# Second block of a two-block kernel: halves of turned columns between products, an output product by tiles, and masks between query copies

## The reference

```python
n = _rmsnorm(h, attn_norm[l])
p = n @ w_in                       # token-shifted part, latents, gates
y_a = _rwkv7_time_mix(...) @ w_out_rwkv
y_b = _mla(q_lat, kv_lat, k_pe, ...) @ w_out_mla
merged = jax.nn.sigmoid(gate_a) * y_a + jax.nn.sigmoid(gate_b) * y_b
h = h + merged @ w_out
n = _rmsnorm(h, ffn_norm[l])
h = h + (jax.nn.gelu(conv(n @ w_up_gate)) * (n @ w_up_val)) @ w_ffn_down
```

## Time and profile before

| | |
|---|---|
| median of 3 runs | 2201.04 us (2199.91 to 2202.91) |
| the profiled execution | 2207.04 us, span 2205.2 us |
| TensorE busy | 1902.1 us (86%) |
| VectorE, ScalarE, GpSimd busy | 914.9 (41%), 739.1 (34%), 40.5 (2%) us |
| weights and the rest read | 592 MB, mean 269 GB/s |
| mean granted TensorE clock | 0.945 |

### The profile page before, as it was taken

How to read it: one execution, slowest core, us unless ns; L and a number is a source line. 1 busy time by engine, 2 the same in 40 slices (tenths; PEclk the granted TensorE clock), 3 DMA queues, 4 the chain that set the end, 5 groups by cost and what they waited for, 6 DMA issues and landing times.

```text
span 2205.2 us, 37736 instructions
## 1 busy us (share of the span) xinstructions
PE 1902.1 (86%) x16684; PEld 1289.0 (58%) x16684; DVE 914.9 (41%) x1316; ACT 739.1 (34%) x1043; POOL 40.5 (2%) x65
## 2 busy tenths in 40 slices
PE   7999976667769999876666679999999999999998
PEld 6897322222218896322122239677899885778996
DVE  6445211111106454110110127457677474476774
ACT  5444211111106453211111125425444453264442
POOL 1000000000001000000000000000000000000000
PEclk9999988888889999988888889999999999999999
DMA  9346999999997257999999996022853450237540
GB/s 331 114 154 270 421 428 429 428 429 429 428 418 292 77 191 321 428 428 429 428 428 429 429 404 216 4 105 102 265 189 136 141 201 4 79 115 246 184 174 20
DMA packets 141523, 592.34 MB, mean 269 GB/s; under 512 B 5808, under 2 KB 59264, under 8 KB 116560
## 3 DMA queue, kind: packets, MB, share of 16 engines
q1 hardware_dynamic: 140288, 586.68, 67.1%
q0 software_dynamic: 1104, 3.70, 0.5%
HBM read 589.30 MB, written 1.05 MB: 268 GB/s over the span
## 4 chain that ended last, share of the span: by engine, by line
PE 68%; DMA 24%; DVE 4%; ACT 2%; issue 1%; SPq 1%; DVEq 0%; POOLq 0%; ACTq 0%; POOL 0%
PE ps L600 38%; DMA ring<-in_w_up 24%; PE ps L1269 12%; PE ps L2394 3%; PE ps L939 2%; PE ps L2443 1%; PE ps L1295 1%; PE ps L1305 1%; PE ps L617 1%; DVE ring_lo L576 1%; PE ps L1045 1%; PE ps L1124 1%; PE ps L1149 1%; SPq L808 1%; ACT slab_hi L571 1%
## 5 line engine op out<-in xcount | busy, mean ns | idle before, releaser
L1269 PE MATMUL ps<-ring,area 128*32 128x512 f32 x1888 | 311.0, 726 | 202.2 <-DMA ring<-in_w_up 202.2
L576 DVE TENSOR_TENSOR ring_lo<-ring,slab_hi 128x2048 fp32r<-128x2048 f32 (+1 forms) x138 | 312.0, 2261 | 217.1 <-ACT slab_hi L571 217.0
L571 ACT ACTIVATE slab_hi<-ring 128x2048 fp32r<-128x2048 f32 (+1 forms) x138 | 260.6, 1888 | 274.9 <-PE ps L600 258.6
L1269 PEld LDWEIGHTS ps<-ring,area 128*32 128x32 f32 x1888 | 72.0, 130 | 403.2 <-DMA ring<-in_w_up 233.6
L600 PE MATMUL ps<-hT_hi,slab_hi 128*128 128x256 f32 x832 | 234.4, 282 | 1.6 <-DVE hT_lo L593 1.6
L600 PE MATMUL ps<-hT_hi,ring_lo 128*128 128x256 f32 x832 | 232.9, 280 | 0.0
L600 PE MATMUL ps<-hT_lo,slab_hi 128*128 128x256 f32 x832 | 232.7, 280 | 0.0
L1541 ACT ACTIVATE area<-ps 128x512 f32<-128x512 f32 x32 | 19.1, 597 | 615.2 <-PE ps L1269 615.2
L1917 DVE COPY area<-ps 128x256 f32<-128x256 f32 x32 | 13.6, 425 | 459.0 <-PE ps L1213 459.0
L1295 PE MATMUL ps<-ring,area 128*32 128x512 f32 x992 | 120.0, 606 | 49.7 <-DVE area L1939 32.5
L600 PEld LDWEIGHTS ps<-hT_hi,slab_hi 128*128 128x128 f32 x832 | 156.6, 188 | 2.0 <-DVE hT_lo L593 2.0
(11 more groups left out here) (428 smaller groups left out, 3199.4 us busy)
## 6 DMA issues: line engine op xcount, KB each, us to landing
ring<-in_w_up SPq DMA_DIRECT2D x60, 2048.0 KB, 20.5
ring<-in_w_down SPq DMA_DIRECT2D x60, 2048.0 KB, 25.4
ring<-in_w_gate SPq DMA_DIRECT2D x56, 2048.0 KB, 15.1
ring<-in_w_ffn_up SPq DMA_DIRECT2D x44, 1024.0 KB, 7.8
ring<-in_w_in SPq DMA_DIRECT2D x18, 2048.0 KB, 10.2
ring<-in_w_ffn_down SPq DMA_DIRECT2D x10, 2048.0 KB, 7.8
ring<-in_xattn_w_kv SPq DMA_DIRECT2D x8, 2048.0 KB, 16.8
area<-in_w_gate SPq DMA_DIRECT2D x6, 2048.0 KB, 16.7
```

Source lines behind the costliest of these rows:

```text
L571: return m.nc.scalar.activation(hi, whole, ACT.Copy)
L576: return m.nc.vector.tensor_tensor(lo, whole, hi, ALU.subtract)
L1269: ins = mm(ps[32 * g:32 * g + CAP, 1, :], m.tokT[:, k, :], gate_up[i][:, k % 4, (g % 2) * BANK:(g % 2 + 1) * BANK], start=k == 0, stop=k = ...
```

## The change

It affects only the second block.

1. **Masks.** The four mask copies (with their wait for `bonus_in`) go from behind the squares to between the second and the third query copy on ScalarE.
2. **Branch.** The second branch product (`w_out_rwkv`) is done tile by tile (both contraction halves of one tile, then the next), where before the tiles of the two halves were interleaved at the start.
3. **Merged.** Half 0 of the merged rows is turned before tile 3 of the branch, half 1 between the two token tiles of the first out product. VectorE makes the low columns of half 0 between the third and the fourth merge, and does its low part of the second out half slab ahead of all merges. `merged_T` and `merged_cols_d` get semaphores of their own.
4. **n2.** Half 1 is turned inside the first up product, which is now done in quarters: c = 0 with columns 0 to 3, turning, c = 1 with columns 0 to 3, then c = 0 and c = 1 with columns 4 to 7. It waits column by column. ScalarE does its second high half slab between the column halves.
5. **n1 of layer 1.** Half 0 is turned before the last tile of the last down product of layer 0; half 1 inside the first input product, by the `first_tiles` that layer 0 has. VectorE's low columns of half 0 stand before the last addition into x. `n1_lo` moves to another area, and the slot of the last down slab is given up with half 1.

```diff
@@ allocate
-    m.n1_lo = over("n1_lo", area_at, after_lat + PAIRS * T, KD, T)
+    m.n1_lo = over("n1_lo", extra_at, SLAB // 2, KD, T)
@@ second_columns
-               freed=m.free[PLAN2[W_DN + NDN - 1].slot] if l and half == 0 else None)
+               freed=m.free[PLAN2[W_DN + NDN - 1].slot] if l and half == 1 else None)
@@ tensor_second
-    if l:
-        for half in range(2):
-            second_columns(m, pe, l, half)
...
-        if l == 0 and q == 0:
+        if q == 0:
             first_tiles()
...
-    for h, i in ((0, 0), (0, 1), (1, 0), (1, 1), (0, 2), (1, 2), (0, 3), (1, 3)):
-        if h == 1 and i == 0:
-            pe.wait_ge(*at("branch_lo", l, 4))
-        branch(0, h, i, (m.ya_hi, m.ya_lo))
+    for i in range(4):
+        if i == 3:
+            merged_columns(0)
+        for h in range(2):
+            if i == 0 and h == 1:
+                pe.wait_ge(*at("branch_lo", l, 4))
+            branch(0, h, i, (m.ya_hi, m.ya_lo))
     release.append(W_ORW)
-    for half in range(2):
-        pe.wait_ge(*at("merged", l, 2 * (half + 1)))
-        pe_columns(m, m.xn, s("merged_T"), (2 * half, 2 * half + 1))
...
+            if j == 0 and t == 1:
+                merged_columns(1)
...
-    pe.wait_ge(*at("h_mixed", l))
-    pe_columns(m, m.x, s("n2_T"), (2, 3))
+    def first_up():
+
+        pe.wait_ge(*at("w_lo", l, 1))
+        w = [a.rearrange("p (k n) -> p k n", k=KD) for a in ffn_half(m, l, 0)[:2]]
+        for half in range(2):
+            for c in range(2):
+                if c and half == 0:
+                    pe.wait_ge(*at("h_mixed", l))
+                    pe_columns(m, m.x, s("n2_T"), (2, 3))
+                for k in range(4 * half, 4 * half + 4):
+                    if c == 0:
+                        pe.wait_ge(*at("n2_cols_d", l, k + 1))
+                    first, ins = exact(m, half_bank(m, up_bank(0, 0), c), [a[:, k, c * P:(c + 1) * P] for a in w],
+                                       [a[:, k, :] for a in columns], c == 0 and k == 0, k == KD - 1, skip_group_check=True)
+                    free_released(first)
+        ins.then_inc(s("up_full"), 1)
...
+            if l + 1 < L and r == NF // 2 - 1 and b == order[-1]:
+                second_columns(m, pe, l + 1, 0)
@@ scalar_second
+        if i == 2:
+            masks()
         act.wait_ge(*at("q2_full", l, i + 1))
...
-    act_high_columns(m, act, m.hT_hi, m.par2("ffn_g"), *at("n2_T", l, 0), s("n2_cols_a"))
+    act_high_columns(m, act, m.hT_hi, m.par2("ffn_g"), *at("n2_T", l, 0), s("n2_cols_a"), (0, 1))
     split(1)
+    act_high_columns(m, act, m.hT_hi, m.par2("ffn_g"), *at("n2_T", l, 0), s("n2_cols_a"), (2, 3))
@@ vector_second
     vector_rwkv_out(m, dve, l)
+    split_in(H_OUT2 + 1)
...
+        if i >= 2:
+            merged_low((2 * i - 4, 2 * i - 3))
-    split_in(H_OUT2 + 1)
     split_in(H_OUT2 + 2)
...
+        if l + 1 < L and i == 3:
+            vector_first_low(m, dve, l + 1, (0, 1))
         dve.wait_ge(*at("down_full", l, i + 1))
```

More of the change, by code:

```diff
@@ L349 @@
 group("gn_pe", second=[("gn_full", 2), ("bonus_full", 2), ("var_full", 1), ("gn_wide", 2), ("gateup_full", 2)])
-group("gn_act", second=[("gateup_in", 1), ("gn_sq", 2), ("mask_set", 4), ("gn_root", 1), ("gn_rows", 2), ("y_scaled", PAIRS),
+group("gn_act", second=[("gateup_in", 1), ("mask_set", 4), ("gn_sq", 2), ("gn_root", 1), ("gn_rows", 2), ("y_scaled", PAIRS),
                         ("ya_hi", 2)])
@@ L356 @@
 group("branch_lo", second=[("branch_lo", 4)])
-group("mla_pe", second=[("q2_full", 4), ("kv2_full", 4), ("qk2_T", 8), ("br2_full", 8), ("merged_T", 4), ("out3_half", 1), ("up_full", 2 * NUP), ("dn_half", NF // 2 - 1)])
+group("mla_pe", second=[("q2_full", 4), ("kv2_full", 4), ("qk2_T", 8), ("br2_full", 8), ("out3_half", 1), ("up_full", 2 * NUP), ("dn_half", NF // 2 - 1)])
+group("merged_T", second=[("merged_T", 4)])
 group("half_pe", first=[("half_used", 7)])
@@ L364 @@
 group("mla_act", second=[("q2_rows", 4), ("kv2_rows", 8), ("qk2_cols_a", 4), ("merged_cols_a", 4)])
-group("mla_dve", second=[("qk2_rot", 1), ("qk2_cols_d", 4), ("merged", 4), ("merged_cols_d", 4)])
+group("mla_dve", second=[("qk2_rot", 1), ("qk2_cols_d", 4), ("merged", 4)])
+group("merged_low", second=[("merged_cols_d", 4)])
 group("ffn_base", second=[("up_base", 2 * NUP)])
@@ L2105, in first_tiles @@
     def first_tiles():
-        pe.wait_ge(*at("lead2_lo", 0))
+        pe.wait_ge(*(at("w2_lo", l, 1) if l else at("lead2_lo", 0)))
         w = half2(m, l, 0)[0:2]
@@ L2130, in tensor_second @@
             for k in range(KD):
-                if q == 0 and c == 0 and k % 4 == 0:
-                    pe.wait_ge(*at("n1_cols_d", l, k + 4))
                 first, ins = exact(m, half_bank(m, SHIFT_BANKS[q], c), [a[:, k, c * P:(c + 1) * P] for a in w],
@@ L2176, in tensor_second, with merged_columns @@
     tensor_mla(m, pe, l, used, free_released)
+    def merged_columns(half):
+        pe.wait_ge(*at("merged", l, 2 * (half + 1)))
+        pe_columns(m, m.xn, s("merged_T"), (2 * half, 2 * half + 1))
     def branch(j, h, i, columns):
@@ L2234, in tensor_second @@
             q = 2 * j + g
+            if q == 0:
+                first_up()
+                continue
             pe.wait_ge(*at("w_lo", l, q + 1))
@@ L2240, in tensor_second @@
                 for k in range(KD):
-                    if q == 0 and c == 0 and k % 4 == 0:
-                        pe.wait_ge(*at("n2_cols_d", l, k + 4))
                     first, ins = exact(m, half_bank(m, up_bank(j, g), c), [a[:, k, c * P:(c + 1) * P] for a in w],
@@ L2800, in scalar_second @@
         scalar_routed(m, act, L - 1, 1)
+    else:
+        split_in(1)
     act_high_columns(m, act, m.n1_hi, first_gain(m, l), *at("n1_T", l, 0), s("n1_cols_a"), (2, 3))
-    split_in(1)
     if l == 0:
+        split_in(1)
         scalar_between(m, act)
@@ L2863, in scalar_second, with masks @@
         go(m.latT[:, c, :], half_bank(m, 2 + c // 2, c % 2), ACT.Copy, scale=gain).then_inc(s("l_cols"), 1)
+    def masks():
+        act.wait_ge(*at("bonus_in", l))
+        for dst, src, scale in ((m.ident_r[:, :], m.ident, 1.0), (m.causal_r[:, 0, :], m.ident, 0.0),
+                                (m.causal_r[:, 1, :], m.const("causal"), 1.0),
+                                (m.of_head, m.ident[:, 0:P:CH // 2].unsqueeze(2).to_broadcast([P, 2 * PAIRS, HD]), 1.0)):
+            go(dst, src, ACT.Copy, scale=scale).then_inc(s("mask_set"), 1)
     for i in range(4):
         t, c0, c1 = i // 2, (0, BANK)[i % 2], (BANK, MH * QKD)[i % 2]
+        if i == 2:
+            masks()
         act.wait_ge(*at("q2_full", l, i + 1))
@@ L2872, in scalar_second @@
         go(m.LW[:, 2 * b:2 * b + 2, :], m.y[:, 2 * b:2 * b + 2, :], ACT.Square, scale=HD ** -0.5).then_inc(s("gn_sq"), 1)
[L2874 to L2878, removed]
     for i in range(4):
@@ L3144, in spread @@
         ins.then_inc(s(done), 1)
-    dve_low_columns(m, dve, m.n1_lo, m.n1_hi, first_gain(m, l), *at("n1_cols_a", l, 0), s("n1_cols_d"), (0, 1))
     if l == 0:
+        vector_first_low(m, dve, l, (0, 1))
         vector_routed(m, dve, L - 1, 1)
@@ L3150, in vector_second @@
         low(m, *lead2_rows(m, 1)).then_inc(s("w2_lo"), 1)
-    dve_low_columns(m, dve, m.n1_lo, m.n1_hi, first_gain(m, l), *at("n1_cols_a", l, 0), s("n1_cols_d"), (2, 3))
+    vector_first_low(m, dve, l, (2, 3))
     split_in(1)
@@ L3210, in vector_second, with merged_low @@
     vector_rwkv_out(m, dve, l)
+    split_in(H_OUT2 + 1)
+    def merged_low(banks):
+        for b in banks:
+            dve.wait_ge(*at("merged_cols_a", l, b + 1))
+            two_k = slice(2 * b, 2 * b + 2)
+            v.tensor_tensor(m.hT_lo[:, two_k, :], two(ps[:, b, :]), m.hT_hi[:, two_k, :], ALU.subtract).then_inc(s("merged_cols_d"), 1)
     dve.wait_ge(*at("gates_sig", l))
@@ L3288, in vector_second, with vector_first_low @@
             vector_split2(m, dve, l + 1, 0)
+def vector_first_low(m, dve, l, banks):
+    dve_low_columns(m, dve, m.n1_lo, m.n1_hi, first_gain(m, l), *m.at("n1_cols_a", l, 0), m.s("n1_cols_d"), banks)
 def vector_split2(m, dve, l, q):
```

## The result

The changed kernel takes 2189.37 us (median of 5 runs, 2188.18 to 2190.65) against 2201.04 us before: ratio 0.9944, 95% interval 0.993 to 0.9959. That is 11.7 us less; 10.45 us and 2190.6 us were forecast. The profiled execution took 2190.65 us with a span of 2188.8 us, 16.4 us less than the profiled execution of before. A second set of runs gave 0.9954 (0.9938 to 0.9971).

A forecast was written before the change was run, and what follows sets the result against it. TensorE was taken to bound the kernel (68% of the span), so edits pay only where it stands still. Gains of 2.0 + 3.9 + 3.9 + 0.65 = 10.45 us off 2201.04 gave 2190.6 us, range 2186.5 to 2196.0.

The forecast's parts named there:

- Place 1: Mask copies moved into ScalarE's hole before the third query copy: 1.0 us per layer, 2.0 us in all, bounds 0 and 2.2.
- Place 2: Merged rows between branch and out products: halves turned without a stall, 1.95 us per layer, 3.9 in all, bounds 0 and 4.2.
- the 1529.6: Sign at the merged rows: VectorE's merges starting later than this, in the before kernel's frame, would show the forecast wrong.
- Place 3: n2, half 1 turned inside the first up product: 1.95 us per layer, 3.9 in all, bounds 0 and 4.8.
- Place 4: Boundary between layers 0 and 1, n1 halves turned inside products: 0.65 us once, bounds -0.5 and 1.5.
- three new waits: Sign at the layer boundary: TensorE would newly wait 0.4 to 0.7 us on n_lo, x and ring_lo.
- SP's slot: Last down slab's slot given up 3.4 us later on SP's queue: hidden by 6 us of slack, otherwise costing up to 3.4.
- A: At n2 and the layer boundary VectorE's low slab eats the gain, leaving 5.9 us: 2195.1 us, chance 0.14.
- B: SP's later slot for the last down slab isn't hidden and costs 3.4 us: 2194.0 us, chance 0.04.
- D: Clock falls at the new hand-overs, 2.2 us each, seven of them making the kernel slower: 2206.0 us, chance 0.03.
- C: Layer 1 starts some 6 us earlier and misses a clock fall of at most 2.2 us: 2188.0 us, chance 0.11.

The follow-up runs named there:

- no_n1: Changed kernel with both halves of n1 turned behind layer 0's last down product again, n1_lo staying in its new area: ratio 0.9958 to the kernel before.
- finer_n1: Changed kernel with the layer boundary cut finer: x completed between VectorE's low columns of banks 0 and 1, half 1 turned after two column blocks: 2192.11 us, ratio 0.9953.
- no_masks: Changed kernel with the mask copies back behind the squares on ScalarE: 2195.38 us, ratio 0.9966 to the kernel before.
- high_back: Changed kernel with only ScalarE's second high half slab of the up weights back behind all high columns: n2 stretch 17.14 and 17.40 us (changed kernel 16.19 and 16.43).
- old_order: Changed kernel with only the second branch product's tile order as before: branch to n2 transposes 41.42 and 41.06 us (changed kernel 40.81 and 40.79).
- late_slot: Changed kernel, larger dose of slot delay: last down slab's slot given up with layer 1's third input product: input products 33.16 us against 31.89.
- no_merged: Changed kernel with branch tile order, turning of merged halves, low columns and VectorE's out slab as before: 2196.19 us, ratio 0.9977 to the kernel before.
- no_n2: Changed kernel with n2 half 1 turned ahead of the whole first up product, four-column waits and ScalarE's old order: ratio 0.9979 to the kernel before.

## Why the prediction was right

Forecast 2190.6 us, measured 2189.37; by steps, per place, forecast against the trace:

- **Place 1**: 2.0 against 2.2 us. I took 1.0 of the 1.12 us, for the second key/value product would be late. It was ready; TensorE's third started 1484.45 - 1482.23 = 2.22 us behind the first pair, where it was 1489.02 - 1485.69 = 3.33, and all of the masks' time came back.
- **Place 2**: 3.9 against 3.8 us. The rebuilt times, shifted by the 4.57 us by which layer 0's branch starts earlier than before (chain: 1515.50 and 1510.93), hold within 0.2 us but for the first merge: merge 3 was to end at 1537.2 and ended at 1532.67 + 4.57 = 1537.24; the low columns were to be in time by 0.1 us, and no wait shows. The first merge started at 1525.14 + 4.57 = 1529.71, just past the 1529.6 that I had named as a sign of being wrong, and ended at 1532.1 and not at 1531.6, for a hole of 0.44 us in VectorE's stream. The sign was set too tight: the next merge waited 0.29 us for TensorE all the same.
- **Place 3**: 3.9 against 4.0 us. Here I had named what would be late next, VectorE's low slab behind the low columns. It is: 1562.70 to 1564.91 on the chain of after, then the second up product. The wait was forecast at 0.5 us; the profile lists 0.16, from a modelled end, and by the starts it is some 0.3. The second up product started at 1564.96 + 6.42 = 1571.4 in the frame of before (where the n2 transposes stand 6.42 us later), against 1571.5.
- **Place 4**: 0.65 against 0.5 us, small for the reason given: the addition that completes x takes the place of the stall. VectorE ends it at 1747.85, TensorE turns half 1 at 1747.90. Of the three new waits that I had named at the boundary, n_lo shows (0.53 us), ring_lo is 0.11 us in the listing (0.3 by the starts) and x is none. The finer cut confirms the reason and shows that moving the addition up gives 0.4 us more; the wait on n_lo stays.
- **SP's slot**: cost nothing, as forecast, with more slack than I gave it. The 11.7 us for a landing in my sum were not the time of the load that matters (see the larger dose).
- **Rivals**: A fell: VectorE is last at places 3 and 4 but takes 0.3 us at the one and some 1 us at the other (n_lo 0.5, the addition 0.4), not the whole. B fell by a dose four times as large that cost 1.27 us. D fell: no clock fall at the places in any profile. The one that came partly true is C, and not for the reason I gave.

C was about layer 1's recurrence. The granted clock there (busy us of PE, PEld, DVE, ACT, POOL; clock, DMA share, GB/s), first two stretches of before, then one of after:

```profile
1836.00:1839.00 3.00, 3.00 (x5) 1.19 (x4) 0.71 (x1) 3.00 (x3) 0.00 (x0) 0.58 0.02 5
1878.00:1881.00 3.00, 3.00 (x14) 2.39 (x14) 1.29 (x2) 0.34 (x2) 0.00 (x0) 0.52 0.03 5
```

```profile
1869.00:1872.00 3.00, 3.00 (x133) 2.45 (x132) 0.61 (x1) 0.00 (x0) 0.00 (x0) 0.61 0.00 0
```

In this stretch before had two falls to 1.2 GHz and after one; the prediction knew of the first alone. Over the thirteen profiles the count is 0, 1 or 2 and follows no edit: the kernel before had two and then one, the kernel after one and then none, `no_n1` and `finer_n1` two, `no_masks`, `high_back` and `old_order` none. The stretch takes 151.7 to 152.1 us where there is none (leaving out `late_slot`), 150.8 to 152.8 with one, 154.1 to 155.0 with two. That is not the falls alone: the chain also has 2.5 to 5.0 us of "issue" gaps here, which differ from run to run too. Less these gaps, it is 147.6 to 147.8 us with no fall, 148.3 to 148.9 with one and 150.1 to 150.3 with two. So of the 2.4 us of the profiled pair the second fall makes some 1.4 and shorter gaps 1.1 (4.85 against 3.79 us). C's gain is a throw of the dice, and I was wrong to tie it to the earlier start.

Each profile has two longer "issue" gaps in that stretch, of 0.8 to 2.1 us, among or just behind products of 32 x 32 tiles. 24 of these 26 gaps are of 1.2 us or more; all 11 falls came inside one of them or within 1.5 us of its end, 13 others had none, nor had the two shorter ones. In layer 0's recurrence, ahead of the first norm sum, five of the profiles (`no_merged`, `no_n2`, `no_n1`, `finer_n1` and, twice, `high_back`) show a fall as well, each behind a gap of 1.8 to 2.2 us. None came at the stalls of 0.3 to 1.4 us between full 128 x 128 products. What decides whether a gap is followed by a fall stays open; no edit here does. The Trainium skill (TensorE: Matmul & The Clock Gate, "A second HAM failure mode: psum-queue depth-cycling") has short idles between groups of matmuls drive the clock down; here that holds in part: falls came behind some of the gaps in the recurrence and at none of the hand-overs of places 1 to 4, with or without the change.

Of the 11.7 us between the medians, 10.5 are shown by place and the other 1.2 are within what the runs differ by; the second set gave 10.7, and 12.5 against the kernel before in its second set (2203.39).

## What to carry to other kernels

Where one engine turns, a second copies and a third subtracts before the first can go on, set half of the turning inside the products before it and half inside the products behind; but look at once for the next thing queued on the subtracting engine, since here half to two thirds of the gain hung on moving one weight slab out of the way (1.3 of 1.9 us, 0.96 of 2.0 us). Rebuild such a place from the starts of instructions and the queue orders, not from the waits that the profile lists, which understate it. Weigh edits of a microsecond by stretches between fixed instructions, which repeat within 0.05 us where whole runs of one kernel differ by 2 to 10.

## What I had not expected of the hardware

- Stretches in which nothing waits for a DMA, outside the recurrence, repeat within 0.05 us or little more over thirteen profiles (174.13 to 174.14 us for the up and down products of layer 0), while the part ahead of them moves by 7.7 us (1475.2 to 1482.9).
- A gap in an engine's own instruction stream can come and go with the order of its instructions: VectorE's hole of 0.44 us between the drain and the sum of its first merge in layer 0 stands in all nine profiles of kernels that do the slab ahead of the merges, and in none of the other four (0.07 us there). It costs only where nothing covers it.
- 2048 KB loads issued 0.4 us apart landed in 9.19 and 14.24 us before, and in 7.95 and 13.19 us in `late_slot`: a median over both is the time of neither, and slack figured from it was too small.
- Falls of the clock and "issue" gaps in the recurrence differ from execution to execution of one kernel, by 0.8 us (changed kernel) and 2.3 us (before) between two profiles of that stretch.
